# A four-layer block on one core: an SSD scan without a state, its decay masks from picks of running sums, its products in place

## What is computed

```
a_cs = cumsum(dt * a_neg)                       # per head, in chunks of 128 tokens
cb = C B^T                                      # per group of 8 heads, 128 x 128
y_diag = (cb * exp(a_cs[l] - a_cs[s]) for l >= s) @ (xs * dt)
state  = B^T (exp(a_cs[last] - a_cs) * xs * dt) # what chunk 0 hands to chunk 1
y_off  = exp(a_cs) * (C state)                  # only chunk 1 has one
y = rmsnorm_per_group((y_diag + y_off + d_skip * xs) * silu(z))
```

## Time and profile before

| | |
|---|---|
| median of 3 runs | 873.74 us (873.58 to 873.85) |
| profiled execution | 873.88 us, its span 872.1 us |
| TensorE (matmul) busy | 861.9 us, 99% |
| VectorE busy | 562.4 us, 64% |
| ScalarE busy | 509.8 us, 58% |
| GpSimd busy | 121.9 us, 14% |
| granted TensorE clock, mean | 0.999 |
| scan of the first hybrid layer | about 290 to 330 us of the span |
| scan of the second | about 619 to 659 us |

### The profile page before, as it was taken

The page is one execution under the profiler, slowest core; times in us unless marked ns, Lnnn a source line. Parts: engine busy times, 40 slices in busy tenths (PEclk is TensorE's granted clock), DMA queues, the critical chain, the costliest instruction groups (busy, mean ns, idle before and its releaser), DMA issues.

```text
span 872.1 us, 12071 instructions
## 1 busy us (share of the span) xinstructions
PE 861.9 (99%) x4426; PEld 702.8 (81%) x4426; DVE 562.4 (64%) x991; ACT 509.8 (58%) x907; POOL 121.9 (14%) x99
## 2 busy tenths in 40 slices
PE   8999999999999999999999999999999999999996
PEld 5877888778888878888888888888878888888885
DVE  6966866677766777755555446576778655555444
ACT  6668466765886864644444334777865644444332
POOL 0122053110153500000000000153510000000000
PEclk9999999999999999999999999999999999999999
DMA  8823563445533336655555555444345655555531
GB/s 307 281 65 105 187 201 135 147 145 173 175 129 131 129 114 209 209 182 179 187 193 194 193 192 172 151 140 145 99 144 187 211 184 192 193 191 175 194 117 48
DMA packets 94765, 146.15 MB, mean 168 GB/s; under 512 B 6516, under 2 KB 54900, under 8 KB 94708
## 3 DMA queue, kind: packets, MB, share of 16 engines
q1 hardware_dynamic: 92820, 139.52, 48.0%
q0 software_dynamic: 1296, 4.72, 1.5%
q10 hardware_dynamic: 592, 1.15, 0.4%
HBM read 144.32 MB, written 1.05 MB: 167 GB/s over the span
## 4 chain that ended last, share of the span: by engine, by line
PE 93%; DVE 2%; ACT 2%; issue 1%; DMA 1%; SPq 0%; POOLq 0%; POOL 0%; ACTq 0%; DVEq 0%
PE bank L1166 79%; PE bank L1114 7%; PE bank L1317 1%; PE bank L1243 1%; PE bank L1221 1%; PE bank L1218 1%; ACT hyb_E L1559 1%; DMA raw<-in_w_in_a 1%; PE bank L1246 1%; ACT hi L1337 0%; PE bank L1323 0%; DVE hyb_xs L1997 0%; DVE hyb_xs L1989 0%; DVE hyb_xs L1995 0%; DVE hyb_rot L1992 0%
## 5 line engine op out<-in xcount | busy, mean ns | idle before, releaser
L1013 DVE TENSOR_TENSOR lo<-raw,hi 128x1024 fp32r<-128x1024 f32 (+1 forms) x244 | 299.4, 1256 | 101.1 <-ACT hi L1337 98.5
L1337 ACT ACTIVATE hi<-raw 128x1024 fp32r<-128x1024 f32 (+1 forms) x260 | 266.9, 1059 | 109.3 <-PE bank L1166 101.0
L1166 PE MATMUL bank<-hi,xT_hi 128*128 128x512 f32 (+2 forms) x736 | 290.3, 394 | 0.4 <-DVE lo L1667 0.2
L1166 PE MATMUL bank<-hi,xT_lo 128*128 128x512 f32 (+2 forms) x736 | 282.6, 384 | 0.0
L1166 PE MATMUL bank<-lo,xT_hi 128*128 128x512 f32 (+2 forms) x736 | 281.8, 383 | 0.0
L1166 PEld LDWEIGHTS bank<-hi,xT_hi 128*128 128x128 f32 x736 | 138.3, 188 | 30.8 <-issue 4.8
L1166 PEld LDWEIGHTS bank<-hi,xT_lo 128*128 128x128 f32 x736 | 138.2, 188 | 28.2
L1166 PEld LDWEIGHTS bank<-lo,xT_hi 128*128 128x128 f32 x736 | 138.6, 188 | 25.2 <-issue 0.5
L1166 PE MATMUL bank<-hi,hT 128*128 128x512 f32 x352 | 109.6, 390 | 0.0
L1166 PEld LDWEIGHTS bank<-hi,hT 128*128 128x128 f32 x352 | 66.1, 188 | 13.7
L1166 PE MATMUL bank<-lo,hT 128*128 128x512 f32 x176 | 68.5, 389 | 0.0
(11 more groups left out here) (251 smaller groups left out, 941.8 us busy)
## 6 DMA issues: line engine op xcount, KB each, us to landing
raw<-in_w_in SPq DMA_DIRECT2D x26, 1024.0 KB, 5.0
raw<-in_w_gate SPq DMA_DIRECT2D x44, 512.0 KB, 3.7
raw<-in_w_up SPq DMA_DIRECT2D x44, 512.0 KB, 4.7
raw<-in_w_down SPq DMA_DIRECT2D x22, 1024.0 KB, 4.8
raw<-in_w_out SPq DMA_DIRECT2D x20, 1024.0 KB, 5.0
raw<-in_w_in_b SPq DMA_DIRECT2D x10, 1024.0 KB, 5.0
raw<-in_w_in_a SPq DMA_DIRECT2D x7, 1024.0 KB, 7.8
raw<-in_w_in_a SPq DMA_DIRECT2D x4, 256.0 KB, 5.4
```

The source lines that it names most:

```text
L1013: return engine.tensor_tensor(lo[r][:, cols], raw[c.i % RAW][:, cols], hi[r][:, cols].bitcast(F32), ALU.subtract)
L1166: last = nc.tensor.matmul(bank[:, 0:wd], still[a], mv[r][:, off:off + wd], start=c.first and i == 0 and j == 0, stop=c.last and i == len(t ...
L1337: nc.scalar.activation(hi[c.i % SPLIT][:, cols], raw[c.i % RAW][:, cols], ACT.Copy)\
```

## The change

The state is gone. `bback` now multiplies B of chunk 0 with C of chunk 1 (`cross`), and `off` multiplies `cross` with `xgd` directly. The decay masks no longer get a prefill: `picks` holds, for each head, 112 rows by 128 columns in bf16: 96 that choose the head's three parts of the running sums, and 16 that add a mask by blocks of eight columns; `csum` has 16 matching rows and a part for each token chunk. What is left above the diagonal inside a block is cleared by a cb that was multiplied with the triangle (`bback` on VectorE, L1985 of the changed kernel), after a `min` against infinities. `picks` is made once, behind `tables()`. ScalarE writes the exponentials into `MT` itself, VectorE multiplies in place, and there are four buffers. The schedule moves `decay` 0,1, `back` 1, the last four `decay` steps and the norm of group 0. Small tiles move to other addresses.

```diff
-    b = halves(sc, w_in, [(z0 + 512, 512)], do(decay, 0, 0, 0) + do(decay, 0, 0, 1) + do(state, 0),
-               do(back, 1) + do(scanned, 0, 0), do(decay, 0, 1, 0) + do(decay, 0, 1, 1))
+    b = halves(sc, w_in, [(z0 + 512, 512)], do(decay, 0, 0, 0) + do(decay, 0, 0, 1),
+               do(decay, 0, 1, 0) + do(decay, 0, 1, 1) + do(scanned, 0, 0), do(back, 1))
...
-        0: (do(decay, 1, 1, 0) + do(state, 1), do(decay, 1, 1, 1)),
-        1: (do(turn_y, 0, 0) + do(scanned, 1, 1), do(turn_y, 0, 1) + do(decay, 1, 0, 0) + do(decay, 1, 0, 1)),
-        2: (do(scanned, 1, 0) + do(group_norm, 1) + do(next_gain), ()),
+        0: (do(group_mean, 0) + do(decay, 1, 1, 0) + do(decay, 1, 1, 1) + do(group_norm, 0),
+            do(decay, 1, 0, 0) + do(decay, 1, 0, 1)),
+        1: (do(turn_y, 0, 0) + do(scanned, 1, 1), do(turn_y, 0, 1)),
+        2: (do(scanned, 1, 0) + do(group_mean, 1) + do(group_norm, 1) + do(next_gain), ()),
...
-                da = Hb["da"][:, 0, :]
-                nc.tensor.matmul(bank[:, 0:32], upper, da, start=True, stop=True)
-                nc.tensor.matmul(bank[:, 32:64], ones[:, :], da, start=True, stop=True)
...
-                nc.tensor.matmul(bank[0:96, 64:64 + P], Hb["da"][:, :, :].rearrange("p a s -> p (a s)"), upper,
...
+                for m in range(M):
+                    c0, da = SH * m, Hb["da"][:, m, 0, SH * m:SH * (m + 1)]
+                    nc.tensor.matmul(bank[:, c0:c0 + SH], upper, da, start=True, stop=True)
+                nc.tensor.matmul(bank[:, 32:32 + SH], spread(ones[:, :], [P, P]), Hb["da"][:, 0, 0, 0:SH], start=True, stop=True)
+                for m in range(M):
+                    last = nc.tensor.matmul(bank[0:96, 64 + m * P:64 + (m + 1) * P],
+                                            Hb["da"][:, m, :, :].rearrange("p a s -> p (a s)"), upper,
+                                            start=True, stop=True)
...
-                    last = transpose(bank[:, g * P:(g + 1) * P], ct[:, 8 + g, 0:P])
+                    last = nc.tensor.matmul(bank[:, g * P:(g + 1) * P], ct[:, 8 + g, 0:P], ct[:, 10 + g, P:S],
+                                            start=True, stop=True)
...
-                nc.tensor.matmul(bank[:, :], identb[:, :],
-                                 spread(masks[:, M_SCAN:M_SCAN + P].unsqueeze(1), [P, 4, P]), start=True, stop=False)
...
-                    pick = masks[0:96, M_SEL + SH * m + hh:M_SEL + SH * m + hh + 1]
-                    last = nc.tensor.matmul(seg, spread(pick, [96, P]), csum[0:96, :], start=False, stop=i == 3)
+                    last = nc.tensor.matmul(bank[:, i * P:(i + 1) * P], picks[0:KSEL, hh, :], csum[0:KSEL, m, :],
+                                            start=True, stop=True)
...
-                nc.tensor.matmul(bank[:, :], Hb["cT"][:, 10 + s.g, P:S], Hb["st"][:, s.g * 512:(s.g + 1) * 512],
+                nc.tensor.matmul(bank[:, :], Hb["cross"][:, s.g, :], Hb["xgd"][:, s.g * 512:(s.g + 1) * 512],
...
-                if s.i >= 2:
-                    act.wait_ge(sem["decay", "vector"], s.i - 1)
+                if s.i >= 4:
+                    act.wait_ge(sem["diag", "tensor"], s.i - 3)
...
+            copy(picks[0:96, :, :], spread(stage[0:96, c1:c1 + SH].unsqueeze(2), [96, SH, P]))
+            copy(picks[96:KSEL, :, :], spread(stage[0:NB, c0:c0 + P].unsqueeze(1), [NB, SH, P]))
+            copy(csum[96:KSEL, :, :], spread(stage[96:KSEL, c0:c0 + P].unsqueeze(1), [NB, M, P]))\
+                .then_inc(picks_made, 1)
...
-                done(tt(Hb[f"MT{s.i % 2}"][:, :, :], Hb[f"E{s.i % 2}"][:, :, :],
-                        spread(Hb["cb"][:, m, g, :].unsqueeze(1), [P, 4, P]), ALU.mult), s)
+                mt = Hb[f"MT{s.i % 4}"][:, :, :]
+                done(stt(mt, mt, BIG, spread(Hb["cb"][:, m, g, :].unsqueeze(1), [P, 4, P]), ALU.min, ALU.mult), s)
+            elif s.kind == "bback":
+                dve.wait_ge(sem["bback", "tensor"], s.i + 1)
+                done(tt(Hb["cb"][:, :, :, :].rearrange("p m g l -> p (m g) l"),
+                        psum[4 + s.banks[0].at][:, :].rearrange("p (a l) -> p a l", l=P),
+                        spread(upper.unsqueeze(1), [P, 4, P]), ALU.mult), s)
```

More of the change, by code:

```diff
@@ L67 @@
 C_MASK = C_KEEP
[L68 to L70 removed]
+C_BLOCK = C_MASK + 2 * QC
+C_SEL = C_BLOCK + P
+C_ALL = C_SEL + SH
+NB = 16
+KSEL = 96 + NB
 def constants():
@@ L99, in constants @@
             c[:, at:at + P] = np.where(x, 0.0, NEG)
-    c[:, C_MASK + 2 * QC:C_SEL] = np.where(t > u, NEG, 0.0)
-    for part in range(3):
-        c[32 * part:32 * part + 32, C_SEL:] = np.eye(32)
+    for b in range(NB):
+        c[b, C_BLOCK:C_BLOCK + P] = np.arange(P) // (P // NB) == b
+        c[96 + b, C_BLOCK:C_BLOCK + P] = np.where(np.arange(P) < b * (P // NB), NEG, 0.0)
+    for part in range(6):
+        c[SH * part:SH * part + SH, C_SEL:] = np.eye(SH)
     return c
@@ L113, in __init__ @@
                  oev=None, den=None, es=None, z=None, nkv=None, dt=None, kind_of=None, ev=None, rope=None,
-                 layer=None, conv=None, soft=None, sums=None, xback=None, bback=None, state=None,
+                 layer=None, conv=None, soft=None, sums=None, xback=None, bback=None,
                  decay=None, mg=None):
@@ L132, in __init__ @@
         self.layer, self.conv, self.soft, self.sums = layer, conv, soft, sums
-        self.xback, self.bback, self.state, self.decay = xback, bback, state, decay
+        self.xback, self.bback, self.decay = xback, bback, decay
 class Bank:
@@ L571, in decay @@
         scan["decay", g, m, i] = s
[L573 to L577, removed]
     def scanned(g, m):
@@ L586, in scanned @@
             ob = sc.bank()
-            last = sc.step("off", g=g, bank=ob, state=scan["state", g])
+            last = sc.step("off", g=g, bank=ob, xback=scan["xback", g], bback=scan["bback"])
         y = sc.step("join", m=m, g=g, bank=yb, obank=ob, last=last, z=scan["z", g], xback=scan["xback", g])
@@ L591, in scanned, with group_mean @@
             ob.freed = (y, "vector")
+    def group_mean(g):
+        scan["mean", g] = sc.step("meansq", what="y", g=g, of=sc.count["join"])
     def group_norm(g):
-        ra = sc.step("meansq", what="y", g=g, of=sc.count["join"])
-        rb = sc.step("newton", what="y", g=g, before=ra)
+        rb = sc.step("newton", what="y", g=g, before=scan["mean", g])
         scan["y", g] = []
@@ L838, in build @@
     gains = keep("gains", [P, D])
+    rope_at = place[0] + 4 * C_COS
     cst = keep("cst", [P, C_KEEP])
[L840 to L843, removed]
+    masks = keep("masks", [P, 2 * QC], BF16)
+    csum = keep("csum", [P, M, P], BF16)
+    picks = keep("picks", [P, SH, P], BF16)
+    ones = keep("ones", [P, 1])
     junk = keep("junk", [P, 512], BF16)
@@ L901, in plan @@
         if hybrid_:
-            put("probT", [P, 4 * QC], where=b["z_at"] + 512)
+            put("probT", [P, 4 * QC], where=b["z_at"] + 1024)
         e = put("k", [P, M, nkv, HD])
@@ L931, in plan @@
             put("xg", [P, M, SSM])
+            e = rope_at
             for name in ("dtr", "dt", "sa", "sb", "sc", "sd"):
[L933 to L937, removed]
+                e = put(name, [P, M, SH], where=e)
+            e = small_at
+            for name, n in (("ncs", M), ("dif", 1), ("dec", 1), ("ecs", 1)):
+                e = put(name, [P, M, SH] if n == M else [P, SH], where=e)
         return b
@@ L1291, in _ @@
                 last.then_inc(sem["xback", "tensor"], 1)
-            elif s.kind == "state":
-                ended(pe, s.xback, "gpsimd")
-                ended(pe, s.bback, "scalar")
-                bank = freed(pe, s.bank)
-                nc.tensor.matmul(bank[:, :], Hb["bt"][:, s.g, :], Hb["xgd"][:, s.g * 512:(s.g + 1) * 512],
-                                 start=True, stop=True).then_inc(sem["state", "tensor"], 1)
             elif s.kind == "decay":
@@ L1316, in _ @@
                     c0 = (4 * (s.q % 2) + i) * HD
-                    last = nc.tensor.matmul(bank[:, c0:c0 + HD], Hb[f"MT{s.decay.i % 2}"][:, i, :],
+                    last = nc.tensor.matmul(bank[:, c0:c0 + HD], Hb[f"MT{s.decay.i % 4}"][:, i, :],
                                             Hb["xg"][:, s.m, hh * HD:(hh + 1) * HD], start=True, stop=True)
```

67 lines of the change are left out of this document (31 added, 36 removed).

## The result

| | before | changed |
|---|---|---|
| median, us | 873.88 (6 runs, 873.58 to 874.81) | 881.68 (6 runs, 879.11 to 882.71) |
| ratio of the changed kernel | | 1.0084, 95% interval 1.0074 to 1.0095 |
| profiled execution, us (span) | 873.88 (872.1) | 880.92 (879.1) |

The forecast was 873.8 us, within 869.8 to 875.9. First its page, parts 1 and 2: busy us, share and instructions of TensorE, and the granted clock in 40 slices.

What follows compares the result with a forecast made beforehand. TensorE was taken to bound the kernel, its saved 6.3 us nearly all lost to waits on other queues: -0.3 us in each of two layers, +0.64 for the picks, sum 0.0, so 873.8 us against the median; range 869.8 to 875.9.

Steps and rivals of the forecast that it cites:

- TensorE's work, -6.3 us: Both hybrid layers: mask prefills and state matmuls go, `bback` and `sums` grow; 3.1 us less a layer, 6.3 in all.
- The picks, a wait of 0.64 us: One-time casts on VectorE: 2.5 us against 1.86 us of idle time, so TensorE waits 0.64 us for the scores.
- `diag` 0,0, a wait of 1.3 us: Hybrid layer's first product: the queue making `MT` is no shorter, so TensorE waits 1.3 us; Z2a starts at 297.5.
- the quarter, 1.9 us: Group 0's norm, now behind two decay products: first quarter ready at 317.8 us, TensorE wants it at 315.9, waits 1.9 us.
- The contention: GpSimd's second x runs beside VectorE's join of 0,1: two instructions take 1.05 us for 0.69, +0.7 us in all.
- the wait of 4.1 us: Wait for the quarter if VectorE and GpSimd lock each other out for whole instructions, 1.4 us each of two.
- What is late next, a layer better by 0.75 us less 0.44: After the quarter: waits of 0.5 us at O2b and 0.2 at group 1's norm; each layer nets -0.3 us.
- Behind it TensorE's own work bounds, as before.: After group 1's norm in each layer: TensorE's work sets the time as before, with no further gain or loss counted.
- The casts at one column per cycle: Rival, slower: both casts of the picks slow, 3.0 us of wait for 0.64, giving 876.2 us; chance 0.1.
- GpSimd held up one instruction and not two: Rival, slower: GpSimd costs the join of 0,1 1.4 us twice, 2.1 us more a layer, 878.0 us; chance 0.07.
- the change did what it says: Rival denied this: a decay step still waits for a buffer, or second x is late; 874 to 876 us, chance 0.03.
- The first rival: Faster: the norm's queue is shorter, TensorE never waits for the quarter; 868.6 us without the waits; chance 0.2.

Runs made afterwards that it cites:

- experiment 8: Changed kernel with 32 unused bytes ahead of `hT`, second x put back ahead of `diag` 0,0 and group 0's norm ahead of `decay` 1,1: 870.97 us, ratio 0.9966.
- Experiment 5: Changed kernel with 32 unused bytes ahead of `hT`, TensorE's waits at group 0's first quarter and `diag` 0,0 filled with matmuls: 874.97 us, ratio 1.0014.
- experiments 1 and 2: 32 bytes left unused ahead of `hT`, in the changed kernel (876.60 us, ratio 1.0049) and in the kernel before (876.75 us, ratio 1.0032).
- experiment 6: Changed kernel with 32 unused bytes ahead of `hT`, only group 0's norm put back ahead of `decay` 1,1: 873.41 us, ratio 0.9996.
- experiment 7: Changed kernel with 32 unused bytes ahead of `hT`, only the second x put back ahead of `diag` 0,0: 872.73 us, ratio 0.9987.
- experiment 2: Kernel before the change with 32 bytes left unused ahead of `hT`, nothing else: 876.75 us, ratio 1.0032.

## Why the prediction was wrong

- **TensorE's work, -6.3 us.** Right: 5.9 us less in experiment 8, where neither the clock nor `hT` adds to it.
- **The picks, a wait of 0.64 us.** Right: 0.7 us, the casts 1.22 us each, at the lower bound. The Trainium skill, Vector Engine (DVE) Microarchitecture Reference, section 5.1, spoke for that bound; the trace agrees with 0.6 ns a column for an operand whose element is read 128 times.
- **`diag` 0,0, a wait of 1.3 us; the quarter, 1.9 us.** Right in the main: 1.16 and 1.87 us. But the sixteen matmuls of `diag` 0,0 then took 2.14 us for 1.73, as the second product came 1.03 us behind the first, so Z2a stood 1.6 us later than the work alone and not 1.3. The contention was counted as 0.36 us twice and was 0.79 us once (1.48 us for 0.69). GpSimd's last instruction for the second x ran from 309.38 to 310.42 us, so the join's third instruction (from 309.49 us) met it and the fourth (from 311.01 us) did not. The Trainium skill, SBUF — State Buffer, section SBUF: two separate sides, has an exclusive lock for a whole instruction. The trace agrees for the one instruction that met GpSimd and doesn't test it on a second; the wait of 4.1 us did not come because there was only one meeting.
- **What is late next, a layer better by 0.75 us less 0.44.** Nearly right. From `bback` to O2b the second hybrid layer of the changed kernel gained 0.54 us, and 0.30 at the first turn behind it (669.25 - 664.12 = 5.1 against 5.4). That is 0.45 us a layer less than forecast, most of the remainder of about 1 us; some 0.3 us of it is the `diag` 0,0 of the point above.
- **"Behind it TensorE's own work bounds, as before."** This step failed, twice. It took TensorE's durations to be fixed by instruction and shape. First, the waits that were forecast do more than last: in the profiled execution the clock behind them fell to half for 6.8 us, 2.8 us on top of the waits. The other five executions have mean clocks of 0.992 to 0.995 where the kernel before has 0.997 to 0.999, which points to such stretches in them too. Experiment 5 shows it by filling them. Second, 528 matmuls in a part that the diff doesn't name became longer by where their stationary operand lies, 3.1 us of busy time, shown in both directions by experiments 1 and 2. The sum had both terms at nothing.
- **Rivals.** The casts at one column per cycle did not come, GpSimd held up one instruction and not two, and the change did what it says. The first rival, no wait for the quarter, came only once the norm was put back, at 873.41 us in experiment 6, and at 870.97 us with the second x put back too, where 868.6 was forecast. No rival named a change in what one matmul takes.

The profiled execution closes: 873.9 forecast, +3.1 for `hT`, +2.8 for the clock, +0.9 for the two scans, makes 880.7; it took 880.92. With 3.4 us for `hT`, as from start to start, it would be 881.0. The median of the six is 0.8 us above this execution.

The change as a whole had a gain in it. Its arithmetic and its early decay steps are worth 3.7 us (870.18 against 873.84) when two of its moves are taken back, the casts stand where VectorE is idle, and `hT` stays at a multiple of 128 bytes.

## What to carry to other kernels

In these kernels a wait of TensorE cost its own length and the risk that the clock fell to half behind it; so an order that leaves idle stretches of 1 to 2 us can be dearer than the chain of waits says, and work moved into such a stretch was worth more than its length (3.9 us for 1.7 in experiment 7). When a change adds or resizes a buffer that stays, compare the addresses of all that lies behind it, and compare the median duration of each group of matmuls, the untouched ones too, before explaining a difference by the edit. When only one engine's work is cut, look for the step whose operands must come sooner, or the time comes back as waits.

## What the runs showed of the hardware that was not expected

- The 128x512 matmuls with `hT`, their stationary operand, took 394 to 398 ns each for 389 where `hT` starts 32, 64 or 96 bytes past a multiple of 128, and 228 of them 53.2 us for 51.7, in three orders of the steps. Other groups whose operands moved by the same bytes kept their lengths (experiment 2), so the runs show it for this group alone. The weight loads have the same length by the trace (187 or 188 ns), so where the time goes isn't shown. The Trainium skill, SBUF — State Buffer, section Operand start alignment, asks only for a multiple of the element's size, and says that this is about legality and not speed; the runs show a cost in speed that it has no word on.
- TensorE's granted clock fell from 1.00 to 0.50 behind idle stretches of 1.1 to 1.9 us, and once behind 0.36 and 0.63 us close together, in an engine busy for 98% of the span. The Trainium skill, TensorE: Matmul & The Clock Gate, section A second HAM failure mode: psum-queue depth-cycling, tells of a clock that falls by frequent small idle stretches. The trace agrees that short ones can do it; here they weren't frequent: two in a layer, 22 us apart, in the changed kernel.
- How long the clock stayed low differed between executions of one program (3.4 or 6.8 us, in one layer or both), with the waits the same to 0.1 us. So the spread between runs rose from 1.2 to 5.6 us, and a wide spread is a sign to look at the clock.
